# An encoder trunk's first mixer: attention output with queries on partitions, and neighbourhood steps moved in among the value blocks

## What is computed

```python
qa, ka, va, qb, kb, vb = split_cols(h @ w_in, [512, 512, 512, 512, 512, 512])
# differential attention, 4 heads, two maps of 64 channels each, values of 128 channels
p = softmax(s)                                  # for both maps m = 0, 1
w = p[map 0] - lam * p[map 1]
o = w @ va                                      # 512 queries x 128 channels a head
oa = rmsnorm(o, subln_g) * (1 - lam_init)       # over the 128 channels of a head
# neighbourhood attention, 8 heads of 64 channels, grid of 8 rows x 64 columns
s = qb . kb / 8 + bias, only 8 x 16 neighbours;  ob = softmax(s) @ vb
x = x + concat(oa, ob) @ w_out
```

## Time and profile before

| what | us |
|---|---|
| median of 3 runs | 1958.45 (1956.9 to 1958.61) |
| profiled execution, its own time | 1959.18 |
| its span, first to last instruction | 1957.4 |
| PE busy / DVE / ACT / POOL in the span | 1891.2 / 1348.5 / 906.3 / 243.1 |
| mean granted TensorE clock | 0.988 of 2.4 GHz |

### The profile page before, as it was taken

How to read it: one execution, slowest core, us unless ns; L and a number is a source line. 1 busy time by engine, 2 the same in 40 slices (tenths; PEclk the granted TensorE clock), 3 DMA queues, 4 the chain that set the end, 5 groups by cost and what they waited for, 6 DMA issues and landing times.

```text
span 1957.4 us, 31136 instructions
## 1 busy us (share of the span) xinstructions
PE 1891.2 (97%) x11220; PEld 1654.4 (85%) x11220; DVE 1348.5 (69%) x1894; ACT 906.3 (46%) x1521; POOL 243.1 (12%) x208
## 2 busy tenths in 40 slices
PE   6999999998989999999999999999999999999996
PEld 5899988776868889998888999888776788999885
DVE  6789843566779579884357888525785677888424
ACT  4455523427347535553243555324377543555322
POOL 2100000213213210000021000001156221000001
PEclk9999999999989999999999999999999999999998
DMA  4232332322210222323222233332321022333321
GB/s 154 68 121 92 108 128 86 101 87 54 72 60 27 81 87 95 120 86 129 98 79 103 87 107 107 111 104 86 113 72 34 23 77 84 108 107 107 113 102 43
DMA packets 36204, 177.14 MB, mean 91 GB/s; under 512 B 12688, under 2 KB 13072, under 8 KB 15520
## 3 DMA queue, kind: packets, MB, share of 16 engines
q1 hardware_dynamic: 33696, 172.55, 26.0%
q10 hardware_dynamic: 2240, 2.98, 0.4%
q0 software_dynamic: 192, 0.59, 0.1%
HBM read 174.01 MB, written 2.10 MB: 90 GB/s over the span
## 4 chain that ended last, share of the span: by engine, by line
PE 90%; DVE 5%; ACT 2%; POOL 1%; issue 1%; DMA 0%; POOLq 0%; ACTq 0%; DVEq 0%
PE ps L308 29%; PE ps L310 28%; PE ps L309 28%; PE ps L1419 1%; DVE wl L278 1%; DVE xgl L356 1%; ACT wh L274 1%; PE ps L1442 1%; PE ps L1049 1%; POOL xg L2225 1%; DVE small L1005 0%; PE ps L1180 0%; PE ps L997 0%; POOL acc L390 0%; PE ps L979 0%
## 5 line engine op out<-in xcount | busy, mean ns | idle before, releaser
L308 PE MATMUL ps<-xgh,wh 128*128 128x256 f32 (+1 forms) x1504 | 514.7, 342 | 24.2 <-DVE xgl L356 13.8
L310 PE MATMUL ps<-xgh,wl 128*128 128x256 f32 (+1 forms) x1504 | 505.8, 336 | 0.0
L309 PE MATMUL ps<-xgl,wh 128*128 128x256 f32 (+1 forms) x1504 | 505.7, 336 | 0.0
L278 DVE TENSOR_TENSOR wl<-raw,wh 128x2048 fp32r<-128x2048 f32 (+1 forms) x93 | 215.0, 2312 | 355.6 <-ACT wh L274 355.6
L308 PE MATMUL ps<-tmh,wh 128*128 128x256 f32 (+1 forms) x1344 | 414.3, 308 | 0.0
L309 PE MATMUL ps<-tml,wh 128*128 128x256 f32 (+1 forms) x1344 | 414.3, 308 | 0.0
L310 PE MATMUL ps<-tmh,wl 128*128 128x256 f32 (+1 forms) x1344 | 414.3, 308 | 0.0
L274 ACT ACTIVATE wh<-raw 128x2048 fp32r<-128x2048 f32 (+1 forms) x93 | 176.5, 1897 | 356.6 <-PE ps L310 355.4
L308 PEld LDWEIGHTS ps<-xgh,wh 128*128 128x128 f32 x1504 | 286.8, 191 | 60.0 <-issue 18.9
L309 PEld LDWEIGHTS ps<-xgl,wh 128*128 128x128 f32 x1504 | 286.9, 191 | 30.4 <-issue 2.9
L310 PEld LDWEIGHTS ps<-xgh,wl 128*128 128x128 f32 x1504 | 286.6, 191 | 29.7
(11 more groups left out here) (284 smaller groups left out, 2599.8 us busy)
## 6 DMA issues: line engine op xcount, KB each, us to landing
raw<-in_units SPq DMA_DIRECT2D x161, 1024.0 KB, 4.9
x<-in_xT ACTq DMA_DIRECT2D x4, 512.0 KB, 7.7
outT<-x SPq DMA_DIRECT2D x8, 256.0 KB, 2.1
relb<-in_rpb SPq DMA_DIRECT2D x64, 24.0 KB, 2.2
cosA<-in_rope_a ACTq DMA_DIRECT2D x1, 256.0 KB, 2.6
sinA<-in_rope_a ACTq DMA_DIRECT2D x1, 256.0 KB, 2.9
cosD<-in_rope_d POOLq DMA_DIRECT2D x1, 256.0 KB, 3.2
sinD<-in_rope_d POOLq DMA_DIRECT2D x1, 256.0 KB, 3.0
```

Source lines behind the costliest of these rows:

```text
L278: nc.vector.tensor_tensor(wl[:, c % 2, 0:n], raw[:, c % 2, 0:n], wh[:, c % 2, 0:n].bitcast(F32), ALU.subtract).then_inc(w_lo, 1)
L308: nc.tensor.matmul(dst, lh, rh, start=first, stop=False, skip_group_check=onto)
L309: nc.tensor.matmul(dst, lh, rl, start=False, stop=False, skip_group_check=onto)
L310: return nc.tensor.matmul(dst, ll, rh, start=False, stop=last, skip_group_check=onto)
```

## The change

It does seven things; no transfer is issued, moved or taken away.

1. The factor becomes -lam * sum0/sum1 and the two maps are combined in one DVE operation, map 0 plus factor times map 1, one step earlier (tile i-1 in step i). POOL's multiplication goes. The missing 1/sum0 is applied by ACT when it copies the product out of PSUM.
2. The product with the values takes the turned weights `aT` as stationary operand and streams 128 columns of `va`, one tile at a time in each step, so queries lie on partitions (`oq`), 16 products in place of 8.
3. The norm is per partition: 16 squares on ACT that also give their sums, one square root and one reciprocal of 16 columns, 16 scalings on ACT, then 16 turns on PE after block 5 and four copies on ACT that apply the gain. The sums with ones, the four wide square roots and the four wide DVE reciprocals and scalings go.
4. The first neighbourhood steps are written out among blocks 9, 10 and 11 (`na_start_pe` and the matching orders on ACT and DVE); the blocks of values from 9 on write bank 7, their turned forms banks 2, 6, 6 and 7.
5. Bias and maximum become one DVE operation for each tile (`tensor_tensor_reduce`, which writes the negated sum and the minimum over it); the exponential takes scale -1.
6. POOL scales both tiles of `pN`, DVE none.
7. The pieces of the output projection start at step i = 6: four in steps 6 and 7, then two a step, four in step 18 (`WO_STEPS`, `WO_READ`). A weight unit that POOL splits is split two steps later.

The diff, cut to its core (the functions that are only lifted out of `na_pe`, `na_act` and `na_dve`, such as `na_turn_pe`, `na_values_pe`, `na_hi_act`, `na_lo_dve`, `na_rec_dve`, `na_out_dve`, have the bodies of before with the waits of their new places):

```diff
+        def vt_pe(pe, i):
+            pe.wait_ge(qb32_done, i + 1)
+            if i >= 10:
+                pe.wait_ge(vb_lo, i - 8)
+            for t in range(TT):
+                mm = nc.tensor.transpose(ps[:, vt_bank(i), t * P:(t + 1) * P],
+                                         qb32[:, i % 2, t * P:(t + 1) * P], ident[:, :])
+            mm.then_inc(vt_done, 1)
...
-                u = (i - 3) // 2
-                if i % 2 == 0 and 0 <= u < 8:
-                    a = u // 2
-                    pe.wait_ge(at_done, 2 * u + 2)
+                u = i - 3
+                if 0 <= u < 16:
+                    a = u // 4
+                    pe.wait_ge(at_done, u + 1)
                     if u >= 2:
                         pe.wait_ge(oa_done, u - 1)
                     for k in range(TT):
-                        mm = nc.tensor.matmul(ps[:, 6 + u % 2, 0:2 * P], va[:, k, a * P:(a + 1) * P], aT[:, u % 2, k, :],
+                        mm = nc.tensor.matmul(ps[:, 6 + u % 2, 0:P], aT_of(aT, u)[:, k, :], va[:, k, a * P:(a + 1) * P],
...
-                u = (i - 4) // 2
-                if i % 2 and 0 <= u < 8:
+                u = i - 4
+                if 0 <= u < 16:
                     act.wait_ge(pa_done, u + 1)
-                    nc.scalar.activation(oA[:, u // 2, 2 * P * (u % 2):2 * P * (u % 2 + 1)],
-                                         ps[:, 6 + u % 2, 0:2 * P], ACT.Copy).then_inc(oa_done, 1)
+                    nc.scalar.activation(oq[:, u // 4, u % 4 * P:(u % 4 + 1) * P], ps[:, 6 + u % 2, 0:P], ACT.Copy,
+                                         scale=col(C_REC + 2 * u)).then_inc(oa_done, 1)
...
-        def diff_pool(pool):
-            for j in range(16):
-                pool.wait_ge(reca_done, 2 * j + 2)
-                nc.gpsimd.tensor_tensor(eA[:, j % 3, 1, :], eA[:, j % 3, 1, :],
-                                        col(C_CF + 2 * (j % 2)).broadcast_to([P, SEQ]), ALU.mult).then_inc(map2_done, 1)
...
-            nc.vector.reciprocal(col(C_REC + b, 2), col(C_SUM + b, 2)).then_inc(reca_done, 1)
+            nc.vector.reciprocal(col(C_REC + 2 * j, 2), col(C_SUM + b, 2)).then_inc(reca_done, 1)
             dve.wait_ge(reca_done, 2 * j + 1)
-            nc.vector.tensor_tensor(col(C_CF + b), col(C_REC + b + 1), col(C_NLAM),
-                                    ALU.mult).then_inc(reca_done, 1)
+            nc.vector.scalar_tensor_tensor(col(C_CF + b), col(C_SUM + b), col(C_NLAM), col(C_REC + 2 * j + 1),
+                                           ALU.mult, ALU.mult).then_inc(reca_done, 1)
         def diff_comb_dve(dve, j):
-            b = 2 * (j % 2)
-            dve.wait_ge(map2_done, j + 1)
-            nc.vector.scalar_tensor_tensor(eA[:, j % 3, 0, :], eA[:, j % 3, 0, :], col(C_REC + b),
-                                           eA[:, j % 3, 1, :], ALU.mult, ALU.add).then_inc(wa_done, 1)
+            dve.wait_ge(reca_done, 2 * j + 2)
+            nc.vector.scalar_tensor_tensor(eA[:, j % 3, 0, :], eA[:, j % 3, 1, :], col(C_CF + 2 * (j % 2)),
+                                           eA[:, j % 3, 0, :], ALU.mult, ALU.add).then_inc(wa_done, 1)
...
-        def diff_norm_pe(pe, a):
...
-        def diff_norm_act(act, a0):
...
-        def diff_sqrt_act(act, a0):
...
-        def diff_norm_dve(dve, a):
...
+        def oq_tile(z):
+            return oq[:, z // 4, z % 4 * P:(z % 4 + 1) * P]
+        def diff_squares_act(act, z0, z1):
+            for z in range(z0, z1):
+                act.wait_ge(oa_done, z + 1)
+                nc.scalar.activation(oA[:, z // 4, z % 4 * P:(z % 4 + 1) * P], oq_tile(z), ACT.Square,
+                                     accum_out=col(C_OSQ + z)).then_inc(ssa_done, 1)
+        def diff_sqrt_act(act):
+            act.wait_ge(ssa_done, 16)
+            nc.scalar.activation(col(C_OSQ, 16), col(C_OSQ, 16), ACT.Sqrt, bias=col(C_EPS),
+                                 scale=1.0 / P).then_inc(arms_done, 1)
+        def diff_rstd_dve(dve):
+            dve.wait_ge(arms_done, 1)
+            nc.vector.reciprocal(col(C_OSQ, 16), col(C_OSQ, 16)).then_inc(rsa_done, 1)
+        def diff_scale_act(act):
+            act.wait_ge(rsa_done, 1)
+            for z in range(16):
+                nc.scalar.activation(oq_tile(z), oq_tile(z), ACT.Copy, scale=col(C_OSQ + z)).then_inc(osc_done, 1)
+        def diff_turn_pe(pe):
+            for a in range(4):
+                pe.wait_ge(osc_done, 4 * a + 4)
+                for t in range(TT):
+                    mm = nc.tensor.transpose(ps[:, 4 + a, t * P:(t + 1) * P], oq_tile(4 * a + t), ident[:, :])
+                mm.then_inc(ot_done, 1)
+        def diff_out_act(act):
+            for a in range(4):
+                act.wait_ge(ot_done, a + 1)
+                nc.scalar.activation(oA[:, a, :], ps[:, 4 + a, :], ACT.Copy, scale=vec(V_SUB)).then_inc(oan_done, 1)
...
+        def na_start_pe(pe):
+            pe.wait_ge(qb_lo, 8)
+            pe.wait_ge(oan_done, 4)
+            na_scores_pe(pe, 0)
+            na_scores_pe(pe, 1)
+            vt_pe(pe, 8)
+            na_block_pe(pe, 9)
+            na_turn_pe(pe, 0)
+            na_scores_pe(pe, 2)
+            vt_pe(pe, 9)
+            na_block_pe(pe, 10)
+            na_turn_pe(pe, 1)
+            na_scores_pe(pe, 3)
+            na_values_pe(pe, 0)
+            vt_pe(pe, 10)
+            na_block_pe(pe, 11)
+            na_turn_pe(pe, 2)
+            na_scores_pe(pe, 4)
+            na_values_pe(pe, 1)
+            vt_pe(pe, 11)
+        WO_STEPS = [0, 0, 4] + [8 + 2 * k for k in range(11)] + [32]
+        WO_READ = (7, 8, 10, 12, 14, 16, 18, 19)
...
-            nc.vector.tensor_tensor(sB[:, i % 2, :, :], ps[:, 4 + i % 2, :].rearrange("p (s k) -> p s k", s=2),
-                                    bm[:, both, h, :, :].rearrange("p s j c -> p s (j c)"),
-                                    ALU.add).then_inc(SN["scores_read"], 1)
-            dve.wait_ge(SN["scores_read"], i + 1)
-            nc.vector.tensor_reduce(col(C_NMX + b, 2), sB[:, i % 2, :, :], AX, ALU.max,
-                                    negate=True).then_inc(SN["max"], 1)
+            biased = bm[:, both, h, :, :].rearrange("p s j c -> p s (j c)")
+            for t in range(2):
+                ins = nc.vector.tensor_tensor_reduce(sB[:, i % 2, t, :], ps[:, 4 + i % 2, 256 * t:256 * t + 256], biased[:, t, :],
+                                                     -1.0, 3.0e38, ALU.add, ALU.min, col(C_NMX + b + t))
+            ins.then_inc(SN["scores_read"], 1)
...
-                    nc.vector.tensor_scalar(na_window(j, t), na_window(j, t), rec[:, t:t + 1], None,
-                                            ALU.mult).then_inc(n_norm, 1)
...
-                t = 1 - j // 8
                 pool.wait_ge(SN["rec"], j + 1)
-                nc.gpsimd.tensor_tensor(na_window(j, t), na_window(j, t),
-                                        recs[:, 2 * (j % 2) + t:2 * (j % 2) + t + 1].broadcast_to([P, 8 * WIN]),
-                                        ALU.mult).then_inc(n_norm2, 1)
+                for t in range(2):
+                    nc.gpsimd.tensor_tensor(na_window(j, t), na_window(j, t),
+                                            recs[:, 2 * (j % 2) + t:2 * (j % 2) + t + 1].broadcast_to([P, 8 * WIN]),
+                                            ALU.mult).then_inc(n_norm2 if na_tile(j, t)[0] else n_norm, 1)
...
-            for i in range(1, 13):
-                if i < 12:
-                    na_block_pe(pe, i)
...
+            for i in range(1, 9):
+                na_block_pe(pe, i)
+                if i == 5:
+                    pe.wait_ge(at_done, 16)
+                    pe.wait_ge(oa_done, 16)
+                    diff_turn_pe(pe)
+            na_start_pe(pe)
             na_pe(pe)
...
+            split_hi(act, BE + 11)
+            vb_hi_act(act, 8)
+            na_exp_act(act, 0)
+            na_exp_act(act, 1)
+            na_hi_act(act, 0)
+            na_exp_act(act, 2)
+            split_hi(act, BE + 12)
+            vb_hi_act(act, 9)
+            na_hi_act(act, 1)
+            na_exp_act(act, 3)
+            vb_hi_act(act, 10)
+            na_hi_act(act, 2)
+            na_exp_act(act, 4)
+            vb_hi_act(act, 11)
+            na_hi_act(act, 3)
+            na_out_act(act, 0)
+            for a in range(4):
+                act.wait_ge(oan_done, a + 1)
+                act.wait_ge(w_half, 2 * (BE + 12))
+                nc.scalar.activation(xgh[:, a, :], oA[:, a, :], ACT.Copy).then_inc(mix_hi, 1)
...
+            split_lo(dve, BE + 11)
+            evac(8)
+            na_max_dve(dve, 0)
+            na_max_dve(dve, 1)
+            vb_lo_dve(dve, 8)
+            na_rec_dve(dve, 0)
+            na_rec_dve(dve, 1)
+            evac(9)
+            na_max_dve(dve, 2)
+            na_lo_dve(dve, 0)
+            split_lo(dve, BE + 12)
+            vb_lo_dve(dve, 9)
+            evac(10)
+            na_rec_dve(dve, 2)
+            na_max_dve(dve, 3)
+            na_lo_dve(dve, 1)
```

(50 more changed lines are left out.)

302 lines of the change are left out of this document (120 added, 182 removed).

## The result

| | before | after |
|---|---|---|
| median, us | 1957.68 (1955.95 to 1958.61, 4 runs) | 1937.52 (1934.78 to 1939.11, 4 runs) |
| profiled execution, its own time | 1959.18 | 1939.11 |
| its span | 1957.4 | 1937.3 |

What follows compares the result with a forecast made beforehand. PE, busy 97% of the span, was taken as the bound. Gains of 2.9 (differential), 2.2 (blocks) and 11.6 (opening) sum to 16.7 us, 1959.2 to 1942.5 profiled, median 1941.8; 8-in-10 range 1935 to 1952.

Steps and rivals of the forecast that it cites:

- differential step: First mixer's differential stage: PE's step 2.52 against 2.645, product 0.95, DVE's combination off the chain; 1.6 us over 13 steps.
- differential stage: First mixer's differential steps and their end before block 0: 1.6 us from steps plus 1.3 at the end, together 2.9.
- block stage: First mixer's value blocks: 16 turns replace four sums with ones, 1.4 us, and a shorter product, 0.8; together 2.2.
- new stall: Opening, behind block 11: PE idles some 3.1 us as product 2 waits for step 0's output split on DVE.
- opening and the rest of the mixer: First neighbourhood steps among blocks 9 to 11: lost 15.2 us less the 3.1 stall and 0.5 late, gain 11.6.
- rival (c): Idle time moves instead of going: product loads at 1.32 take 4.8, opening gains only 2; 1955 to 1959 us; chance 0.09.
- Rival (b): Opening stays chained: PE waits 2 to 3 us behind each of blocks 9, 10, 11; 1949 us; chance 0.15.
- rival (a): Clock also falls in the new stall: 4 us at 1.2 GHz gives 1944, 8 gives 1946; chance 0.20.
- The prediction's own sign for being wrong: Longer wait at the first product behind block 11 or any turn, clock low over 5 us, or steady steps changing length.
- Fused operation: Bias and maximum in one DVE operation per tile: 0.9 us for two tiles; counting as four instructions might leave no gain.
- Steady steps: Neighbourhood steps after the opening: PE busy throughout, nothing gained, again 4.09 us; POOL's step grows to 3.4.
- rival (d): Slower: POOL bounds the steady steps if its 3.4 grows past 4.09; 1964 us at 2 us excess a step; chance 0.06.

Runs made afterwards that it cites:

- experiment 5: Changed kernel with the differential combination put back one step later on VectorE, POOL multiplying the second map again; 1937.34 us, ratio 0.9899.
- experiment 6: Changed kernel with bias and maximum put back to two operations, an addition and a maximum for both tiles; 1939.86 us, ratio 0.9904.
- experiment 2: Changed kernel with small again 88 columns wide, its 48 new columns in a tile at the end of the mixer's memory; 1940.89 us, ratio 0.9898.
- experiment 9: Kernel before with an unused tile of 48 columns ahead of all others, moving every tile 192 bytes; 1952.56 us (one run).
- experiments 1, 7 and 8: Kernel before with small 136, 104 and 120 columns wide instead of 88, no instruction changed; 1953.88, 1961.16 and 1964.11 us.
- experiments 2, 3 and 9: Changed kernel, small 88 wide: 1940.89 us; changed kernel, opening's old order put back: 1946.36; kernel before, unused 48-column tile in front: 1952.56.

## Why the forecast was right, and where it was not

The faster side and most of the mixer's gain followed from the steps named. That the median came within 4.3 us of the forecast is in part luck, as two errors had opposite signs: the mixer gave 14.0 and not 16.7, and 6.1 came from outside it, for a reason that the forecast did not have. In the profiled executions 1942.5 stood against 1939.1.

| term | forecast | measured |
|---|---|---|
| differential step | 2.52 (product 0.95) | 2.37 (product 0.89) |
| differential stage | 2.9 | 3.3: block 0 starts 5.5 earlier (490.46, 484.92), of which 2.2 were there at scores 2 |
| block stage, block 0 to block 8 | 2.2 (turns 2.0) | 2.6 (turns 1.75) |
| new stall | 3.1 | 2.55 |
| opening and the rest of the mixer | 11.6 | 8.1 (14.0 - 3.3 - 2.6); some 12 without the price of the fall, 3.9 to 4.2 |
| feed-forward blocks | 0 | 5.45 |

**Differential steps.** Right: no wait for DVE, and two steps in 4.75 us. The product was mis-sized by 0.06 (0.89 is close to half of 1.73) and the turn by as much (0.59), and the fear that the eight weight loads would bound the product, on which rival (c) rested, did not come true. The reason given is not borne out for the loop. The step says that the wait goes because the combination leaves DVE's chain; experiment 5 puts the combination back and the steps stay at 2.37. For the tail it is: 1.3 were forecast, and the combination was measured to be worth 1.7 there.

**Block stage.** Right, and undersized by 0.4: 16 turns in one row took 1.75, 0.11 each, where the forecast went from 0.66 for a row of four. The scalings took 4.78 us of ACT (5.1 forecast) and were hidden by blocks 4 and 5.

**Opening.** The order did what was worked out for it: each turn behind blocks 9, 10 and 11 without a wait, one stall where it was placed and with the releaser it was given. Rival (b) is out. The step that failed is the one that holds the clock at full speed in that stall: rival (a), given 0.20, happened in the profiled execution. It was priced at 4 us for 8 us at the lower level; 10.2 us cost 3.9 and 4.2 in two comparisons. The prediction's own sign for being wrong, over 5 us at the lower level, is met. That it need not fall there is shown by experiment 5, with the same stall and no fall. The Trainium skill, "TensorE: Matmul & The Clock Gate", section "HAM oscillation — how this bites in real kernels", has idle gaps between bursts drop the clock again and again; the profiles agree that such a gap can, and show one that did not.

**Fused operation.** 0.42 and a read of 0.08, but 0.34 from one to the next, so 0.69 a step, and not 0.9: below the lower bound given, as the read and the next operation overlap. The Trainium skill, "VectorE: DVE Perf Modes", section "Two Vector instructions with no wait between them", counts two instructions, a main one and a read; the trace agrees on the count, and the fear that this eats the gain is not borne out: 0.69 for both tiles stands against 0.69 + 0.69.

**Steady steps.** Right: 4.09, with 0.7 less or more of DVE work (experiment 6). POOL took 0.61 a tile and the splits 1.29; rival (d) is out.

**The layout.** The missing term. Some 5.5 us came from a line of the diff that reads as bookkeeping, 48 columns added to `small`. The forecast counted instructions; this made some 3,000 matmuls 2% shorter and some 2,000 2% longer. Without it the change is worth about 14 us by experiment 2's marks, some 3 less than was forecast (that kernel's median is lower still, and its profile shows a shorter second mixer); with it and without the fall of the clock it would be near 24.

**Open.** Which pair of tiles matters at which distance was not settled: only all tiles behind `small` were moved against all ahead of it. Nor was it settled what decides whether the clock falls in a given stall, and for how long. It is not the instructions alone: the first mixer of the kernel before, with its tiles in several places, shows 13.7 us at the lower level in experiment 9, 17.1 in the first profile and 20.5 in experiments 1, 7 and 8, with a mixer of 294.2, 295.2 and 296.2 to 297.0 us. So the missing fall of experiment 5 need not be due to its edit. The second mixer, untouched, took 222 to 223 us in three profiles (experiments 2, 3 and 9), none of which shows a fall of the clock there, and 225 to 228 in the others, all of which do; that is more than the spread within most sets of runs.

## What to carry to other kernels

Lay the new order of each queue against the others with the durations of the old trace: here it placed the one new stall within a microsecond and named the releaser, which then was the next thing to mend (one output split moved up in two queues, 6 us). A stall in a kernel that keeps PE full costs its length and, sometimes, more than that again for the lower clock behind it: 2.55 and about 4 here. And compare stretches whose code is the same before reading a result: when they differ, look at what moved in memory, since a wider tile can be worth as much as a stage rewritten.

## What the runs showed that was not expected

- The rate of matmuls with 128 x 128 weights depends on the distance between tiles, for 256 moving columns otherwise than for 512: a feed-forward stretch took 347.7, 348.7, 349.0 and 350.8 to 351.2 at distances of 192, 64, 0 (or 256) and 128 bytes.
- The same 2.55 us of idle PE, behind the same blocks and steps, went with 10.2 us at the lower clock in two kernels (the changed one, experiment 2) and with none in another (experiment 5).
- A DVE operation that adds, reduces and gives its accumulator follows its like after 0.34 us for 256 columns, as fast as half an addition over 512 (0.69).
